# The six up-projection units of a hybrid block as three rounded products, with the branches' rows rounded straight from PSUM

## The reference

```python
y_ssm = s5_branch(u_ssm, ...)             # 256 x 512, a state-space scan
y_dsa = dsa_branch(q, k, v, qi, ki, wi, positions)   # 256 x 512, attention over selected keys
y_mem = memory_branch(qm, km, vm)         # 256 x 512, attention over a memory
g_s, g_d, g_m = jnp.split(jax.nn.sigmoid(gates), N_BRANCHES, axis=-1)
merged = g_s * (y_ssm @ w_up_ssm) + g_d * (y_dsa @ w_up_dsa) + g_m * (y_mem @ w_up_mem)
x = x + merged @ w_out
x = x + hier_moe(rms_norm(x, g_ffn), ...)  # 32 experts of 1024 x 512, 2 per token
```

## Time and profile before

| | |
|---|---|
| median of 3 runs | 1992.89 us (1992.08 to 1995.36) |
| the profiled execution | 1996.01 us, span 1994.2 us |
| busy: TensorE, VectorE, ScalarE, GpSimd | 93%, 58%, 41%, 4% of the span |
| mean granted TensorE clock | 0.98 of full |
| HBM read | 557 MB, 280 GB/s over the span |

### The profile page before, as it was taken

How to read it: one execution, slowest core, us unless ns; L and a number is a source line. 1 busy time by engine, 2 the same in 40 slices (tenths; PEclk the granted TensorE clock), 3 DMA queues, 4 the chain that set the end, 5 groups by cost and what they waited for, 6 DMA issues and landing times.

```text
span 1994.2 us, 29944 instructions
## 1 busy us (share of the span) xinstructions
PE 1864.1 (93%) x12352; PEld 1419.6 (71%) x12352; DVE 1149.6 (58%) x1487; ACT 826.0 (41%) x1018; POOL 84.0 (4%) x72
## 2 busy tenths in 40 slices
PE   7999998878778778999999999999999999999998
PEld 5457757544444444788888788888888888788887
DVE  5998357533334334655678386556655688385554
ACT  4336522222212122534467465333534467555331
POOL 2552000000000000000000000000000000000000
PEclk9999999989998899999999999999999999999999
DMA  9369758999999999555454354655646454364652
GB/s 316 103 137 270 213 180 336 400 421 419 420 421 420 420 420 356 201 169 200 150 179 149 126 198 161 211 169 169 216 164 202 160 168 158 117 210 153 207 169 105
DMA packets 166920, 467.03 MB, mean 234 GB/s; under 512 B 9808, under 2 KB 21328, under 8 KB 142080
## 3 DMA queue, kind: packets, MB, share of 16 engines
q1 hardware_dynamic: 152144, 435.07, 59.0%
q0 software_dynamic: 13024, 26.81, 6.0%
q10 hardware_dynamic: 1616, 3.24, 0.5%
HBM read 557.36 MB, written 1.05 MB: 280 GB/s over the span
## 4 chain that ended last, share of the span: by engine, by line
PE 71%; DMA 17%; DVE 7%; ACT 2%; issue 1%; POOL 0%; SPq 0%; ACTq 0%; DVEq 0%
PE ps L1041 21%; PE ps L1051 18%; PE ps L1050 18%; DMA ring<-in_w_down 16%; PE ps L1211 3%; PE ps L1561 2%; PE ps L1543 1%; PE ps L1522 1%; DMA ring<-in_w_up 1%; PE ps L1179 1%; PE ps L1180 1%; DVE xn L2590 1%; DVE W L2595 1%; DVE W L2597 1%; DVE xn L2584 1%
## 5 line engine op out<-in xcount | busy, mean ns | idle before, releaser
L2389 DVE TENSOR_TENSOR w_lo<-raw,w_hi 128x2048 fp32r<-128x2048 f32 x152 | 333.7, 2208 | 126.3 <-ACT w_hi L1856 118.8
L1051 PE MATMUL ps<-w_hi,a_lo 128*128 128x512 f32 (+1 forms) x992 | 374.7, 378 | 0.0
L1856 ACT ACTIVATE w_hi<-raw 128x2048 fp32r<-128x2048 f32 x152 | 279.7, 1849 | 225.9 <-PE ps L1041 193.1
L1041 PE MATMUL ps<-w_hi,a_hi 128*128 128x512 f32 (+1 forms) x928 | 354.1, 382 | 0.2 <-DVEq L2429 0.2
L1050 PE MATMUL ps<-w_lo,a_hi 128*128 128x512 f32 (+1 forms) x912 | 343.3, 376 | 0.0
L1543 PE MATMUL ps<-ring,W 128*32 128x256 f32 x3008 | 189.7, 400 | 56.0 <-DMA ring<-in_w_up 53.3
L1051 PEld LDWEIGHTS ps<-w_hi,a_lo 128*128 128x128 f32 x992 | 186.6, 188 | 35.0
L1041 PEld LDWEIGHTS ps<-w_hi,a_hi 128*128 128x128 f32 x928 | 174.7, 188 | 33.5 <-issue 2.7
L1050 PEld LDWEIGHTS ps<-w_lo,a_hi 128*128 128x128 f32 x912 | 171.8, 188 | 30.4 <-issue 0.2
L1543 PEld LDWEIGHTS ps<-ring,W 128*32 128x32 f32 x3008 | 94.7, 114 | 136.8 <-DMA ring<-in_w_up 63.4
L2389 DVE TENSOR_TENSOR y_lo<-raw,y_hi 128x2048 fp32r<-128x2048 f32 x50 | 114.6, 2292 | 48.4 <-ACT y_hi L1856 45.5
(11 more groups left out here) (468 smaller groups left out, 2846.1 us busy)
## 6 DMA issues: line engine op xcount, KB each, us to landing
ring<-in_w_gate SPq DMA_DIRECT2D x94, 1024.0 KB, 22.1
ring<-in_w_up SPq DMA_DIRECT2D x94, 1024.0 KB, 26.3
ring<-in_w_down SPq DMA_DIRECT2D x94, 1024.0 KB, 21.0
raw<-in_w_in SPq DMA_DIRECT2D x50, 1024.0 KB, 5.1
raw<-in_ffn_w_up SPq DMA_DIRECT2D x44, 1024.0 KB, 5.2
raw<-in_ffn_w_gate SPq DMA_DIRECT2D x42, 1024.0 KB, 5.1
raw<-in_ffn_w_down SPq DMA_DIRECT2D x40, 1024.0 KB, 6.0
raw<-in_w_out SPq DMA_DIRECT2D x10, 1024.0 KB, 5.0
```

Of the source, the lines that this page charges most:

```text
L1041: return released(pe.matmul(dst, a, b, skip_group_check=True, **kw))
L1051: return pe.matmul(dst, a_l, b_h, start=False, stop=final, skip_group_check=True)
L1856: act.activation(E.hi_view(name, ahead), E.raw_view(name, ahead), ACT.Copy).then_inc(hi_split, 1)
L2389: tt(E.lo_view(name, ahead), E.raw_view(name, ahead), E.hi_view(name, ahead).bitcast(F32), ALU.subtract)\
```

## The change

The six up units go the second way: their weights are split like those of `wo`, and the branches' rows are split too. For the attention branches ScalarE rounds the output straight from PSUM (`attended_hi`) into parts of `a_hi` and `a_lo` that are free by then, and VectorE's copy becomes a subtraction of the rounded part (`attended`). The scan branch is rounded from `y_full` and its rest is taken in place (`scan_branch_rest`). The orders of ScalarE and VectorE are rewritten to take the new work in.

```diff
-PRE_SPLIT = [(("wo", c), kh) for c in range(2) for kh in range(2)]
+PRE_SPLIT = [("up", br, c) for br in ("ssm", "dsa", "mem") for c in range(2)] + [(("wo", c), kh) for c in range(2) for kh in range(2)]
...
+        branch_hi = [a_hi[:, 0:4], a_hi[:, 4:8], a_lo[:, 0:4]]
...
             def up(br, c):
-                pe.wait_ge(done["branch"], nth("branch", br if br == "ssm" else (br, 1)))
-                raw_rows([("up", br, c)], [("up", br, c, t) for t in range(2)], y_full[:, ("ssm", "dsa", "mem").index(br)])
+                pe.wait_ge(done["branch"], nth("branch", "ssm_rest" if br == "ssm" else (br, 1)))
+                i = ("ssm", "dsa", "mem").index(br)
+                rows_panel([("up", br, c)], [("up", br, c, t) for t in range(2)], (branch_hi[i], y_hi[:, i]))
...
             def hi1(name):
 
                 n0 = PRE_SPLIT.index(name)
-                if n0 >= RAW:
-                    act.wait_ge(unit_used, E.unit_value(PRE_SPLIT[n0 - RAW]) + 1)
+                earlier = PRE_SPLIT[n0 - RAW] if n0 >= RAW else CAST_UNITS[(7, 10, 11)[n0]]
+                act.wait_ge(unit_used, E.unit_value(earlier) + 1)
...
             gate(4)
+            def attended_hi(tag, t, slot):
+                name = (tag, "O", t)
+                act.wait_ge(bank_filled[bank_of[name]], fills(name))
+                act.activation(branch_hi[slot][:, :, t * P:t * P + P], psum(name).rearrange("p (i s) -> p i s", s=P), ACT.Copy)\
+                    .then_inc(branch_rounded, 1)
+            attended_hi("dsa", 0, 1)
+            act.wait_ge(done["branch"], nth("branch", "ssm"))
+            act.wait_ge(unit_used, E.unit_value((("gate", 4), 1)) + 1)
+            act.activation(branch_hi[0], y_full[:, 0], ACT.Copy).then_inc(branch_rounded, 1)
             for t in range(2):
...
+            hi1(("up", "ssm", 0))
             gate(5)
+            hi1(("up", "ssm", 1))
             probs_out("dsa", 1, 4, probsT)
...
+            hi1(("up", "dsa", 0))
+            attended_hi("dsa", 1, 1)
             probs_out("mem", 0, 2, probsT[:, :, 0:4])
+            hi1(("up", "dsa", 1))
+            attended_hi("mem", 0, 2)
+            probs_out("mem", 1, 2, probsT[:, :, 4:8])
+            hi1(("up", "mem", 0))
+            attended_hi("mem", 1, 2)
+            hi1(("up", "mem", 1))
             hi1((("wo", 0), 0))
-            probs_out("mem", 1, 2, probsT[:, :, 4:8])
...
-            def attended(tag, t, slot):
-                dve.wait_ge(bank_filled[bank_of[(tag, "O", t)]], fills((tag, "O", t)))
+            def scan_branch_rest():
+                dve.wait_ge(branch_rounded, 2)
+                tt(y_hi[:, 0], y_full[:, 0], branch_hi[0].bitcast(F32), ALU.subtract).then_inc(done["branch"], 1)
+                dve.wait_ge(done["branch"], nth("branch", "ssm_rest"))
+            def attended(tag, t, slot, rounded):
+                dve.wait_ge(branch_rounded, rounded)
...
-                dve.tensor_copy(y_full[at], p_).then_inc(bank_freed[bank_of[(tag, "O", t)]], 1)
+                tt(y_hi[at], p_, branch_hi[slot][:, :, t * P:t * P + P].bitcast(F32), ALU.subtract)\
+                    .then_inc(bank_freed[bank_of[(tag, "O", t)]], 1)
```

More of the change, by code:

```diff
@@ L252, in plan @@
     mark("relued", (0, 0), (0, 1), (1, 0), (1, 1))
-    mark("branch", "ssm")
+    mark("branch", "ssm", ("dsa", 0), "ssm_rest", ("dsa", 1), ("mem", 0), ("mem", 1))
     for tag, pairs in (("dsa", 4), ("mem", 2)):
@@ L258, in plan @@
             mark("probs_turned", *((tag, t, p) for p in range(pairs)))
-            mark("branch", (tag, t))
     def small_scores(tag, t, pairs):
@@ L739, in bass_hybrid_moe_then_swa_gla @@
         negated = semaphore("negated")
+        branch_rounded = semaphore("branch_rounded")
         gate_rows_negated = semaphore("gate_rows_negated")
@@ L815, in pre_halves @@
                 nk, w = unit_shape[name]
-                hi, lo = w_hi[:, PRE_SPLIT.index(name) % RAW], pre_raw[self.pre_slot(name)][1]
+                hi, lo = w_hi[:, (PRE_SPLIT.index(name) + 2) % RAW], pre_raw[self.pre_slot(name)][1]
                 return [v[:, 0:nk * w].rearrange("p (k n) -> p k n", n=w) for v in (hi, lo)]
@@ L2807, in _ @@
             normalised("dsa", 1, 4, probs, 0)
-            attended("dsa", 0, 1)
+            attended("dsa", 0, 1, 1)
+            scan_branch_rest()
+            lo1(("up", "ssm", 0))
+            lo1(("up", "ssm", 1))
             for t in range(2):
@@ L2812, in _ @@
                 normalised("mem", t, 2, probs[:, 4 * t:4 * t + 4], 4 * t)
+            lo1(("up", "dsa", 0))
+            attended("dsa", 1, 1, 3)
             weighted_up(0, 0)
-            attended("dsa", 1, 1)
+            lo1(("up", "dsa", 1))
+            attended("mem", 0, 2, 4)
             weighted_up(0, 1)
-            attended("mem", 0, 2)
+            lo1(("up", "mem", 0))
+            attended("mem", 1, 2, 5)
+            weighted_up(1, 0)
+            lo1(("up", "mem", 1))
+            weighted_up(1, 1)
             lo1((("wo", 0), 0))
[L2818 to L2821, removed]
             def by_part(v):
@@ L2831, in _ @@
                 dve.wait_ge(bank_freed[bank_of[name]], fills(name))
+            weighted_up(2, 0)
+            lo1((("wo", 0), 1))
+            weighted_up(2, 1)
             lo1((("wo", 1), 0))
-            weighted_up(2, 0)
-            weighted_up(2, 1)
             turned("m")
```

## The result

The changed kernel took 1997.77 us (median of 20 runs, 1994.67 to 2000.15), the kernel before 1995.26 (20 runs, 1992.08 to 1997.18). The ratio is 1.0013, 95% interval 1.0007 to 1.0019: 2.6 us slower, between 1.4 and 3.8. The forecast was a difference of +0.3 us and a time of 1993.2, at most 1996.3; both are missed. Of the 4.6 us between 1997.77 and 1993.2, 2.4 are the base: the three runs that the forecast stood on had a median of 1992.89, and twenty runs of the same kernel have 1995.26.

What follows compares the result with a forecast made beforehand. TensorE was taken as the bound up to 287.08 us, VectorE from there; -1.3 us on the path and +1.6 for the clock gave +0.3 on a median of 1992.89, so 1993.2 us, range 1990.1 to 1996.3.

Steps and rivals of the forecast that it cites:

- Removed: Six up units on TensorE at 5.5 us each instead of 6.87, saving 8.2 us of its time.
- Steps one and two: Before the memory scores: PSUM bank 0 freed later, +0.45 us; second ssm unit's rounding ahead of turned probabilities, +1.81.
- the bank: PSUM bank 0, freed later for the memory heads' fourth transpose, moves gate panel 5 by +0.45 us.
- Step four: After the sigmoids, rounding, subtractions and gated copies make the first dsa unit start 1.2 us late.
- Step five: From the last branch VectorE's queue of 23.8 us sets the output projection's start: 1.3 us gained of 8.2.
- Step six: Clock falls after waits before the scores and in the tail, each nothing to 1.6 us; half each, 1.6 in all.
- rival B: Both clock falls at full price: -1.3 + 3.2 = +1.9 us, so 1994.8, slower than before; chance 0.27.
- Step seven: Behind 290 us the same instructions follow in the same order, the expert stage passing a shift on: nothing more.

Runs made afterwards that it cites:

- e8: Kernel before with only the two ssm units as three rounded products, their roundings ahead of gate panel 5's copies; 0.9987 of the kernel before.
- e9: Changed kernel with e4's three moves, the second output-projection unit's subtraction and the third's rounding put behind those of the merged rows; 0.9966 of the kernel before.
- e2: Changed kernel with ScalarE's rounding of the second ssm unit moved ahead of gate panel 5's copies; 0.9996 of the kernel before.
- e1: Changed kernel with VectorE's subtraction for the third output-projection unit moved behind the rests of the merged rows; 0.9993 of the kernel before.
- e5: Changed kernel with 3, 3 and 10 spare matmuls in TensorE's three tail waits; 0.9994 of the kernel before.
- e4: Changed kernel with the moves of e1 and e2, and the first dsa unit's rounding moved behind the turned probabilities; 0.9966 of the kernel before.
- c2: The changed kernel run again without an edit; 1.0009 of the kernel before.
- c1: The kernel before run again without an edit; 0.9998 of the kernel before.
- e6: e4 with 3, 3 and 1 spare matmuls in its three remaining tail waits; 0.9954 of the kernel before.
- e3: Changed kernel with 4, 4 and 16 spare matmuls in TensorE's three tail waits; 0.9998 of the kernel before.

## Why the prediction was wrong

**Removed: right.** 5.53 us a unit against the 5.5 forecast; e8 and e9 show that the saving can be had.

**Steps one and two: right.** The scores come 2.27 us later against 2.26 forecast, after a wait of 2.33 against 2.34. e2 takes out 1.80 and leaves 0.47, the bank.

**Step four: nearly.** The first dsa unit starts 44.63 us behind the attention products against 43.04 in the kernel before, so 1.6 late and not 1.2.

**Step five: right.** VectorE's queue from the last branch to TensorE's start is 23.7 us (266.91 to 290.58) against 23.8 forecast; the start is 1.1 us earlier against 1.3. e1 shows the queue to be the bound.

**Step six, the clock: the step that failed.** It put two possible falls at half of 1.6 us each, 1.6 in all. There was one, in the tail, and it cost 2.2, the difference of 18.60 and 16.41; e5 gets 16.44 with everything else in place. The half-clock piece in the tail is longer than the one that I took the price from (0.50 or near it from 288 to 295 us). The rule behind it, that a wait near 2.47 us brings the clock down and one near 1.64 doesn't, was wrong too: a wait of 2.33 in front of the scores left the clock at 1.00, and it fell behind waits of 0.76, 0.80 and some 0.2 with four transposes between one and the next (e1, e4). By the Trainium skill (TensorE: Matmul & The Clock Gate, "HAM oscillation — how this bites in real kernels") waits between bursts let the clock fall and what follows pays half of the throttled time. The tail agrees on the price: 2.2 us of the 4.6 from 290.58 to some 295.2.

**The sum.** With the measured terms it is -1.1 + 2.2 = +1.1 in place of -1.3 + 1.6 = +0.3, and both profiles show that for the stretch: 0.6 of these 0.8 us are step six. As far as the stretch goes, this is rival B by sign and mechanism, with one fall where B had two.

**Step seven, nothing more behind 290 us: not settled.** By the times 1.5 of the 2.6 us lie outside the stretch, in the second comparison 0.8 of 1.8, there within the interval. The profiled executions show no such loss: from the transposes of the next stage to the end of the span it is 1687.5 and 1686.2 us in the kernel before, 1686.1 and 1687.6 in the changed one. In between, the changed kernel gains 1.5 us near 350 us (last section) and has lost it again when the expert stage ends: from the first product on `zero_b`, which follows that stage (790.25 us in the kernel before), to the end of the span all thirteen profiled executions take 1203.5 to 1204.0 us. What the times add beyond the stretch was not caught by a profile, and its cause stays open.

The clock is suspected, not shown. The results give span and mean granted clock of every execution, and (1 - clock) x 2 x span is its time at half clock. The changed kernel has 83.4 us of it (20 executions) and 85.3 (c2's 11); the kernel before has 80.1 (31 that ran beside e1 to e4) and 78.1 (27 beside c1, c2, e5 and e6). Together that is 84.1 against 79.2 (79.4 with the other 36 of the kernel before), and half of the difference is 2.5 us, with a standard error of 0.7: as much as the whole loss. But this doesn't follow the tail from kernel to kernel: e3 and e5, with the tail held, have 78.2 and 78.6, e4, with a fall there, 79.0, and e8, without one, 82.9. Nor does it close. The spans less half of their half-clock time are 1954.0 and 1953.0 against 1953.1 and 1954.3, 1953.6 in both together, where the changed kernel should be some 2 us lower: its path is 1.1 us shorter, and of the 3.4 us that the rows from 288 to 296 us take off for the tail only 2.2 lay on the path. What is shown is that holding the clock in the tail, and nothing else, took 3.0 us (0.4 to 5.6) off the time (e5).

**The base.** A median of three runs stood 2.4 us under that of twenty. The range of 6 us around it held the difference (+2.6), not the time.

## What to carry to other kernels

A cheaper instruction on the bound engine is worth what the queues that feed it can follow: count the new work against the idle time of these engines at its place, and put each piece into a gap or behind the instruction that TensorE waits for. Here the same work, moved by a few lines in two queues, went from 0.13% slower to some 0.4% faster. Short waits in a row can cost twice, once as waits and once through the clock behind them; here spare matmuls in them held the clock, and the stretch was 1.7 to 2.2 us shorter (e6, e5).

## What was not expected

The kernel before has a fall of the clock near 350 us, where the changed kernel has none. TensorE timeline, the same 64 matmuls and the row behind them, kernel before and changed:

```profile
348.57 5.20 PE L1543 MATMUL ps<-ring,W 128*32 128x256 f32 x64 [2.73 <-DVE W L3157]
353.59 1.90 PE L1561 MATMUL ps<-ring,W 128*32 128x256 f32 x32
```

```profile
351.03 3.66 PE L1545 MATMUL ps<-ring,W 128*32 128x256 f32 x64 [2.73 <-DVE W L3193]
354.51 1.91 PE L1563 MATMUL ps<-ring,W 128*32 128x256 f32 x32
```

Both stand behind the same wait of 2.73 us; the kernel before runs them partly at half clock and loses 1.5 us, the changed kernel doesn't. All five profiled executions with a fall in the tail pass this place at 1.00. Of the eight without one, seven fall here and e8 doesn't, so the earlier fall does not decide it alone. To the row behind these matmuls it is 140.37 and 140.46 us from the attention products in the two executions of the changed kernel, 140.80 and 141.15 in those of the kernel before: here the slower kernel is ahead. And e5 stands at 139.93, only 0.4 to 0.5 us ahead of the changed kernel, where its time is 3.0 us shorter. Equal waits at equal places don't fix the clock, and one place in one profile can't tell the sign of a change of this size.
